# RWKV key direction: head norms summed into 16 rows and spread back by a zero-one matrix, b multiplied on GpSimd

## What is computed

```python
a = jax.nn.sigmoid((a0 + (xa @ a1) @ a2).astype(f32))
kk = (k * k_k.astype(f32)).reshape(B, T, RWKV_HEADS, RWKV_HEAD)
kk = kk / jnp.maximum(jnp.sqrt(jnp.sum(kk * kk, axis=-1, keepdims=True)), 1e-12)
k = k * (1.0 + (a - 1.0) * k_a.astype(f32))
...
# in the recurrence: -kk and b = kk * a
```

## Time and profile before

| what | value |
| --- | --- |
| median of 3 runs | 2409.98 us (2407.46 to 2410.36) |
| the profiled execution's own time | 2418.79 us |
| its span, first to last instruction | 2417.2 us |
| mean granted TensorE clock | 0.904 |
| busy in the span: PE, DVE, ACT, POOL | 87%, 41%, 28%, 7% |
| the block of the change in the trace | 1362.1 to 1433.7 us |

### The profile page before, as it was taken

The page is one execution under the profiler, slowest core; times in us unless marked ns, Lnnn a source line. Parts: engine busy times, 40 slices in busy tenths (PEclk is TensorE's granted clock), DMA queues, the critical chain, the costliest instruction groups (busy, mean ns, idle before and its releaser), DMA issues. The chain is left out here.

```text
span 2417.2 us, 51803 instructions
## 1 busy us (share of the span) xinstructions
PE 2112.1 (87%) x20994; PEld 1892.1 (78%) x20994; DVE 995.4 (41%) x1572; ACT 679.9 (28%) x1151; POOL 157.4 (7%) x240
## 2 busy tenths in 40 slices
PE   4599888878889999996699959999996789999995
PEld 4566556666689999996599739999873589999995
DVE  5323432211244333334943385544416643333333
ACT  2112335334223221221532233323201232212222
POOL 0002201333000000000000000000113000000000
PEclk7797899878999999998899759999977799999997
DMA  3022302455222323221132000001001222232311
GB/s 115 13 61 68 117 1 66 135 151 167 77 70 82 101 66 92 84 77 44 45 87 79 10 0 2 0 0 35 1 6 46 70 70 83 82 114 62 100 55 48
DMA packets 255006, 156.02 MB, mean 65 GB/s; under 512 B 24760, under 2 KB 247839, under 8 KB 254752
## 3 DMA queue, kind: packets, MB, share of 16 engines
q1 hardware_dynamic: 234644, 140.07, 19.6%
q10 hardware_dynamic: 14092, 7.95, 1.2%
q0 software_dynamic: 6144, 6.30, 0.9%
HBM read 148.89 MB, written 5.34 MB: 64 GB/s over the span
## 5 line engine op out<-in xcount | busy, mean ns | idle before, releaser
L308 PE MATMUL ps<-ffn_xh,ffn_wh 128*128 128x280 f32 x1408 | 299.1, 294 | 17.5 <-DVE ffn_xl L1394 13.2
L308 PE MATMUL ps<-ffn_xh,ffn_wl 128*128 128x280 f32 x1408 | 297.4, 293 | 0.0
L308 PE MATMUL ps<-ffn_xl,ffn_wh 128*128 128x280 f32 x1408 | 296.5, 292 | 0.0
L308 PEld LDWEIGHTS ps<-ffn_xh,ffn_wh 128*128 128x128 f32 x1408 | 226.1, 190 | 18.5 <-issue 18.3
L308 PEld LDWEIGHTS ps<-ffn_xh,ffn_wl 128*128 128x128 f32 x1408 | 225.8, 190 | 0.0
L308 PEld LDWEIGHTS ps<-ffn_xl,ffn_wh 128*128 128x128 f32 x1408 | 224.8, 190 | 0.0
L1296 ACT CAST ffn_wh<-wa 128x1024 fp32r<-128x1024 f32 x88 | 91.3, 1042 | 206.6 <-PE ps L308 179.5
L308 PE MATMUL ps<-ffn_hid_h,ffn_wh 128*128 128x280 f32 x704 | 148.0, 291 | 0.0
L308 PE MATMUL ps<-ffn_hid_h,ffn_wl 128*128 128x280 f32 x704 | 147.6, 291 | 0.0
L308 PE MATMUL ps<-ffn_hid_l,ffn_wh 128*128 128x280 f32 x704 | 147.5, 291 | 0.0
L314 DVE TENSOR_TENSOR ffn_wl<-wa,ffn_wh 128x1024 fp32r<-128x1024 f32 x88 | 107.6, 1225 | 85.8 <-ACT ffn_wh L1296 85.8
(11 more groups left out here) (356 smaller groups left out, 4000.3 us busy)
## 6 DMA issues: line engine op xcount, KB each, us to landing
wa<-in_ffn_w_gate SPq DMA_DIRECT2D x44, 512.0 KB, 3.6
wa<-in_ffn_w_up SPq DMA_DIRECT2D x44, 512.0 KB, 3.6
arena<-in_cache_latent SPq DMA_DIRECT2D x104, 128.0 KB, 2.1
wb<-in_ffn_w_down SPq DMA_DIRECT2D x16, 768.0 KB, 4.7
wb<-in_ffn_w_down SPq DMA_DIRECT2D x16, 640.0 KB, 4.2
wb<-in_cache_latent SPq DMA_DIRECT2D x73, 128.0 KB, 2.2
wa<-in_attn_w_o SPq DMA_DIRECT2D x8, 512.0 KB, 4.5
wa<-in_rwkv_w_r SPq DMA_DIRECT2D x8, 512.0 KB, 3.6
```

The lines of the kernel that those rows point to most:

```text
L308: mm = nc.tensor.matmul(dst[:, s, 0:HALF], a[:, c * width:(c + 1) * width], b[:, c, s * HALF:(s + 1) * HALF], start=first and n == 0, stop ...
```

## The change

- The square is taken straight from k with the scale k_k (L1671); the separate copy into kk goes.
- The sums of all 16 heads are collected in one tile of 16 rows: for each m a 128 x 16 window of a constant of zeros and ones puts the two heads of m into rows 2m and 2m + 1, and all eight m accumulate in one pair of banks (L1636). All eight go ahead of the other matmuls.
- Maximum, reciprocal and square root are taken once, on 16 x 560 (L1686, L1688, L1679). The square root stands between the sigmoids of m = 2 and m = 3.
- PE spreads the 16 rows back over 128 partitions with a 16 x 1024 matrix of zeros and ones (`spread`, a new input that SP fetches to a free weight buffer), one 16-row matmul per half and m (L1650). Ahead of it the products for the first four m are made; the rest alternate with it.
- DVE makes kk as (k * k_k) * spread in one instruction (L1695), out of PSUM, ahead of the product that overwrites k (L1698).
- b = kk * a is made on GpSimd (L1705).

The diff (the last part, which passes the new input, is left out):

```diff
@@ -71,7 +71,7 @@
 NCON = _at
 
 _at = LATER = CON["causal"][0]
-for _name, _n in [("abrb_t", 2 * L), ("near_t", L), ("owner", DB)]:
+for _name, _n in [("abrb_t", 2 * L), ("near_t", L), ("owner", DB), ("window", 4 * DC - 2)]:
     CON[_name] = (_at, _n)
     _at += _n
 NLATER = _at - LATER
@@ -116,7 +116,10 @@
     ang = (inv[:, None] * pos[None, :]).astype(np.float32)
     put("cos", np.concatenate([np.cos(ang), np.cos(ang)]))
     put("sin", np.concatenate([-np.sin(ang), np.sin(ang)]))
-    return c, later[:, LATER:LATER + NLATER]
+
+    put("window", np.arange(4 * DC - 2)[None, :] == 2 * (DC - 1) + p[:, None] // RH, later)
+    spread = np.repeat(np.eye(2 * DC, dtype=np.float32), RH, 1)
+    return c, later[:, LATER:LATER + NLATER], spread
 
 
 class Ring:
@@ -346,6 +349,11 @@
             dve.wait_ge(cut.slab_done, n + 1)
             x = split(xT[:, n])
             nc.vector.tensor_tensor(x, x, halves(2 * (n % 4)), ALU.add).then_inc(cut.kept, 1)
+
+        def head_window(m):
+
+            a = 2 * (DC - 1) - 2 * m
+            return const("window", P, a, a + 2 * DC)
 
         def ge(eng, s, v):
 
@@ -1602,76 +1610,100 @@
 
 
         sg, kk, av = mixed0, mixed1, xx
-        w2, a2 = wa.buf[0][0:64], wa.buf[1][0:64]
+        w2, a2, spread = wa.buf[0][0:64], wa.buf[1][0:64], wa.buf[2][0:2 * DC]
+        HD = 2 * DC
         sq = wb.buf[0][:, 0:2 * T].rearrange("p (s t) -> p s t", s=2)
         kscale = wb.buf[1][:, 0:2 * T].rearrange("p (s t) -> p s t", s=2)
-        norms = hT
+        inverse = rs[0:HD]
         one_less = wb.buf[1][:, 4 * T:4 * T + DC]
-        l2_in, sw_done, a_done, sw_kept, a_kept = sem("lora2_in"), sem("decay_done"), sem("a_done"), sem("decay_kept"), sem("a_kept")
-        kk_raw, kk_sq, kk_summed, kk_mean, kk_root, kk_done = (sem(f"kk_{n}") for n in ("raw", "squared", "summed", "mean", "root", "done"))
-        k_scaled, b_done, less = sem("k_scaled"), sem("b_done"), sem("one_less")
+        l2_in, spread_in = sem("lora2_in"), sem("spread_in")
+        sw_done, a_done, sw_kept, a_kept = sem("decay_done"), sem("a_done"), sem("decay_kept"), sem("a_kept")
+        kk_sq, kk_summed, kk_mean, kk_root, kk_spread, kk_done = (sem(f"kk_{n}") for n in ("squared", "summed", "mean", "root", "spread", "done"))
+        less, scale_done, k_scaled, b_done = sem("one_less"), sem("k_scale"), sem("k_scaled"), sem("b_done")
+        SUMS_AT, A_AT, W_AT, SPREAD_AT = 0, 2, 4, (6, 0)
         with nc.Block(no_gpsimd_drain=True) as block:
             @block.sync
             def _(sp):
+                sp.dma_start(a2, w["rwkv_a2"][0]).then_inc(l2_in, 16)
                 sp.dma_start(w2, w["rwkv_w2"][0]).then_inc(l2_in, 16)
-                sp.dma_start(a2, w["rwkv_a2"][0]).then_inc(l2_in, 16)
+                sp.dma_start(spread, w["spread"]).then_inc(spread_in, 16)
 
             @block.tensor
             def _(pe):
+                for m in range(DC):
+                    pe.wait_ge(kk_sq, m + 1)
+                    for s in range(2):
+                        mm = nc.tensor.matmul(ps[0:HD, SUMS_AT + s, 0:HALF], head_window(m), sq[:, m % 2, s * HALF:(s + 1) * HALF],
+                                              start=m == 0, stop=m == DC - 1)
+                    mm.then_inc(kk_summed, 1)
+
+                def second(m, bank, src, hid, done, left):
+                    ge(pe, left, m)
+                    for s in range(2):
+                        mm = nc.tensor.matmul(ps[:, bank + s, 0:HALF], src[:, m * P:(m + 1) * P],
+                                              lora[0:64, hid, s * HALF:(s + 1) * HALF], start=True, stop=True)
+                    mm.then_inc(done, 1)
+
+                def spread_out(m):
+                    ge(pe, kk_done, m - 1)
+                    for s in range(2):
+                        mm = nc.tensor.matmul(ps[:, SPREAD_AT[m % 2] + s, 0:HALF], spread[:, m * P:(m + 1) * P], inverse[:, s],
+                                              start=True, stop=True)
+                    mm.then_inc(kk_spread, 1)
+
                 pe.wait_ge(l2_in, 32)
+                FIRST = 4
+                for m in range(FIRST):
+                    second(m, A_AT, a2, 1, a_done, a_kept)
+                    second(m, W_AT, w2, 0, sw_done, sw_kept)
+                pe.wait_ge(spread_in, 16)
+                pe.wait_ge(kk_root, 1)
                 for m in range(DC):
-                    ge(pe, sw_kept, m)
-                    ge(pe, a_kept, m)
-                    for b, src, hid, done in ((0, w2, 0, sw_done), (2, a2, 1, a_done)):
-                        for s in range(2):
-                            mm = nc.tensor.matmul(ps[:, b + s, 0:HALF], src[:, m * P:(m + 1) * P],
-                                                  lora[0:64, hid, s * HALF:(s + 1) * HALF], start=True, stop=True)
-                        mm.then_inc(done, 1)
-                    pe.wait_ge(kk_sq, m + 1)
-                    ge(pe, kk_mean, 2 * (m - 1))
-                    for s in range(2):
-                        mm = nc.tensor.matmul(ps[:, 4 + 2 * (m % 2) + s, 0:HALF], pair, sq[:, m % 2, s * HALF:(s + 1) * HALF],
-                                              start=True, stop=True)
-                    mm.then_inc(kk_summed, 1)
+                    spread_out(m)
+                    if m + FIRST < DC:
+                        second(m + FIRST, A_AT, a2, 1, a_done, a_kept)
+                        second(m + FIRST, W_AT, w2, 0, sw_done, sw_kept)
 
             @block.scalar
             def _(act):
                 for m in range(DC):
-                    nc.scalar.activation(kk[:, m], k[:, m], ACT.Copy, scale=vcol("k_k", m)).then_inc(kk_raw, 1)
-                    act.wait_ge(kk_raw, m + 1)
                     ge(act, kk_summed, m - 1)
-                    nc.scalar.activation(sq[:, m % 2], kk[:, m], ACT.Square).then_inc(kk_sq, 1)
+                    nc.scalar.activation(sq[:, m % 2], k[:, m], ACT.Square, scale=vcol("k_k", m)).then_inc(kk_sq, 1)
+                for m in range(DC):
+                    act.wait_ge(a_done, m + 1)
+                    nc.scalar.activation(split(av[:, m]), halves(A_AT), ACT.Sigmoid, bias=vcol("a0", m)).then_inc(a_kept, 1)
                     act.wait_ge(sw_done, m + 1)
-                    nc.scalar.activation(split(sg[:, m]), halves(0), ACT.Sigmoid, bias=vcol("w0", m)).then_inc(sw_kept, 1)
-                    act.wait_ge(a_done, m + 1)
-                    nc.scalar.activation(split(av[:, m]), halves(2), ACT.Sigmoid, bias=vcol("a0", m)).then_inc(a_kept, 1)
-                for m in range(DC):
-                    act.wait_ge(kk_mean, 2 * m + 2)
-                    nc.scalar.activation(norms[:, m], norms[:, m], ACT.Sqrt).then_inc(kk_root, 1)
+                    nc.scalar.activation(split(sg[:, m]), halves(W_AT), ACT.Sigmoid, bias=vcol("w0", m)).then_inc(sw_kept, 1)
+                    if m == 2:
+                        act.wait_ge(kk_mean, 2)
+                        nc.scalar.activation(inverse, inverse, ACT.Sqrt).then_inc(kk_root, 1)
 
             @block.vector
             def _(dve):
                 ka = vec[:, VEC["k_a"][0]:VEC["k_a"][0] + DC]
                 nc.vector.tensor_scalar(one_less, ka, -1.0, 1.0, ALU.mult, ALU.add).then_inc(less, 1)
+                dve.wait_ge(kk_summed, DC)
+                nc.vector.tensor_scalar(inverse, ps[0:HD, SUMS_AT:SUMS_AT + 2, 0:HALF], 1e-24, None, ALU.max).then_inc(kk_mean, 1)
+                dve.wait_ge(kk_mean, 1)
+                nc.vector.reciprocal(inverse, inverse).then_inc(kk_mean, 1)
                 dve.wait_ge(less, 1)
                 for m in range(DC):
-
-                    dve.wait_ge(kk_summed, m + 1)
-                    nc.vector.tensor_scalar(split(norms[:, m]), halves(4 + 2 * (m % 2)), 1e-24, None, ALU.max).then_inc(kk_mean, 1)
-                    dve.wait_ge(kk_mean, 2 * m + 1)
-                    nc.vector.reciprocal(norms[:, m], norms[:, m]).then_inc(kk_mean, 1)
-
                     dve.wait_ge(a_kept, m + 1)
                     nc.vector.tensor_scalar(kscale[:, m % 2], av[:, m], vcol("k_a", m), one_less[:, m:m + 1], ALU.mult,
-                                            ALU.add).then_inc(k_scaled, 1)
-                    dve.wait_ge(k_scaled, 2 * m + 1)
-                    dve.wait_ge(kk_raw, m + 1)
+                                            ALU.add).then_inc(scale_done, 1)
+                    dve.wait_ge(kk_spread, m + 1)
+                    nc.vector.scalar_tensor_tensor(out=split(kk[:, m]), in0=split(k[:, m]), scalar=vcol("k_k", m),
+                                                   in1=halves(SPREAD_AT[m % 2]), op0=ALU.mult, op1=ALU.mult).then_inc(kk_done, 1)
+                    dve.wait_ge(scale_done, m + 1)
                     nc.vector.tensor_tensor(k[:, m], k[:, m], kscale[:, m % 2], ALU.mult).then_inc(k_scaled, 1)
+
+            @block.gpsimd
+            def _(pool):
                 for m in range(DC):
-                    dve.wait_ge(kk_root, m + 1)
```

(11 more changed lines are left out.)

## The result

The changed kernel takes 2430.36 us (median of 4 runs, 2424.55 to 2445.67), the kernel before 2408.72 (4 runs, 2405.12 to 2410.36). The ratio is 1.0092, interval [1.0052, 1.0132]: slower by 0.9%, where I had forecast 18 us less. The profiled execution took 2425.59 us, with a span of 2423.9.

What follows compares the result with a forecast made beforehand. Three bounds in turn: the fetch of w2 and a2, PE at 1.2 GHz, the DVE tail. Gains of 4.2, 8.9, 9.2 and 14.8 against costs of 4.0 and 14.8 give 18.3 us off 2409.98: 2391.7, range 2387 to 2407.

Steps and rivals of the forecast that it cites:

- the first part: What bounds the old block: weight fetch, PE at 1.2 GHz, DVE tail; any gain comes off the span one for one.
- the next block waits for something that it had for nothing: Rival, behind the block: the change does not do what it says; no gain, 2410 us; 3%.
- Sums first at 2.4 GHz: Block's start: PE begins at 1362.9 instead of 1367.06; eight groups of pair sums at 1.05 us take 8.4 us.
- the slow-clock rival: Whole block at clock 0.50, sums taking 16.2 us; gain only 3.2 us, 2406.8 us; 13%.
- Reciprocal at full length on 16 partitions: After the sums, on DVE: the single reciprocal takes the full 3.65 us, yet stays off the path.
- Root in the middle: Between sigmoids of m = 2 and m = 3: Sqrt and two table loads, no drain; 4.0 us around the root.
- Clock falls near the root and stays at 0.50: Between about 1378 and 1382 PE mostly waits, the clock falls and stays down; rounds take 6.19 us, spreading costs 14.8.
- L1692 beside GpSimd at no cost: Spreading rounds: DVE's scale is not slowed by GpSimd's b; DVE needs 1.95 us per m, b takes 1.36 to 1.43.
- the bounds of 0 and 5: Last four m: us lost in all if DVE's scale had to wait for each GpSimd b; 0 taken, upper bound 6%.
- the low end: Last four m: 0 us lost to GpSimd and DVE slowing each other, since POOL's median beside a busy DVE is 1.36.

Runs made afterwards that it cites:

- the seventh experiment: The changed kernel with 150 padding increments where PE waits anyway, and the square root replaced by a plain copy, so both table loads go: 2388.13 us (one run).
- the eighth experiment: The changed kernel with 150 padding increments where PE waits anyway, and low-rank and spreading matmuls over 128 rows, the added ones zeros: 2380.94 us, ratio 0.9893.
- the first experiment: The changed kernel with 150 semaphore increments on PE right ahead of the recurrence's loop: 2411.03 us, ratio 1.0012.
- the fifth: The changed kernel with 150 semaphore increments where PE waits anyway (25 and 65 in the projections, 60 ahead of the recurrence's loop): 2392.41 us, ratio 0.9940.
- the fourth: The kernel before with 150 semaphore increments on PE right ahead of the recurrence's loop: 2490.05 us, ratio 1.0336.

## Why the prediction was wrong

**The step that failed** is the last sentence of the first part: "A barrier stands between, so what the block gives back comes off the span one for one." It holds for time, and I took it to hold for everything. What the change did outside its block was to shift the code behind it. That the code moves was to be seen before the run: a compiled list can be counted, the page lists the queue of instruction fetches, and the trace shows rounds of 33.5 us without one fetch. What a shift of 52 would cost was not to be seen there. None of my rivals had it; "the next block waits for something that it had for nothing" (3%) comes near its effect, but says nothing of code, and was priced at no gain, not at a loss. It cost 33.0 us, and 34.0 in the kernel before with 52 increments.

**The block, step by step**, in us from its start (1362.1 in my timeline, 1353.1 in the trace):

| step | forecast | measured |
| --- | --- | --- |
| sums done | 9.2 | 8.8 |
| sigmoids of m = 2 done | 16.1 | 15.7 |
| first spreading group starts | 18.1 | 17.8 |
| sigmoid of a, m = 3, done | 20.1 | 19.7 |
| PE's last spreading group done | 51.0 | 50.0 |
| last b done | 53.3 | 55.4 |

- *Sums first at 2.4 GHz*: right. The clock stayed at 1.00 up to 1371, and the slow-clock rival is out.
- *Reciprocal at full length on 16 partitions*: right, 3.64 us against 3.65, and off the path.
- *Root in the middle*: right. The Sqrt starts 1.29 us after its load, as in the earlier trace rows, and the seventh experiment bounds all that the two loads cost at 2.7 us. By the Trainium skill's drain of 1.38 us per switch ("ScalarE: Activation LUTs", "What ACT_TABLE_LOAD costs") it would be 5.3, an estimate from that page's figures; the trace does not show it.
- *Clock falls near the root and stays at 0.50*: right in size, 0.50 from 1380 to 1409 with rounds of 6.19 us as in the earlier trace rows. The reason that I gave for the fall, that PE mostly waits there, is not needed. Without the root PE is busy 8.00 of 8 us and then 10.00 of 10, and the clock falls; with 128 rows PE has the same wait for the root (0.86 us in both), and the clock stays at 1.00 up to 1390. The rule of the Trainium skill ("TensorE: Matmul & The Clock Gate", "What's actually happening"), that activity releases the throttle, does not hold for the low-rank and spreading matmuls of this block. The prediction argued that from rows, and the eighth experiment shows it. Few rows alone do not bring the slow clock either: most matmuls of the recurrence are 64*64, and between 1480 and 1513.5 in the kernel before they run at 1.00, with PE busy 31.99 of 33.5 us. What sets the two apart stays open.
- *L1692 beside GpSimd at no cost*: mis-sized. It takes 1.61 to 1.62 us instead of 0.46, and L1705 1.80 instead of the 1.36 to 1.43 of the earlier trace rows, where GpSimd ran beside other DVE work. Each time L1692 starts 0.5 us behind L1705 and ends 0.3 behind it (1404.28 + 1.61 = 1405.89 beside 1403.78 + 1.80 = 1405.58 above), so it looks like a wait for GpSimd's operation rather than slower work. DVE's 1.95 us per m became 2.89, so in the last four groups DVE and not PE set the pace. Behind PE's last group came 5.4 us instead of 2.3; PE was done 1.0 earlier, and the end came 2.1 us later than forecast. That is within the bounds of 0 and 5 that I had given it; I took the wrong end. The reason that I gave for the low end, POOL's own median beside a busy DVE, said nothing on what DVE loses.

The block took 56.0 us for 53.3 (these 2.1, and 0.6 from the last result to the barrier's end), and with the loop in a good place the kernel took 2392.41 for 2391.7. The model of the block was right, the model of the program was not.

## What to carry to other kernels

A hand-scheduled program has one more resource: the place of its loops in the instruction stream. Where an edit changes the number of instructions ahead of a long loop, compare the packets of the instruction queue and the rounds of the loop before believing any verdict on the edit; if they moved, pad in an idle place on that engine and time again. And look whether matmuls over few rows that run at the slow clock can be filled up with zeros: here that alone took the block from 56.6 to 43.6 us.

## What the runs showed of the hardware that I had not expected

- A loop of 1702 PE instructions runs without a fetch from some places. From others it is fetched again in every second round (32 us over eight rounds) or in every round (72 us). The refetch stalls PE for 3.3 to 4.5 us at the jump back, and behind it the clock is at 0.50 for some 10 to 14 us.
- A semaphore increment on PE takes 0.152 us from start to start. I had counted on a third of it, the 0.051 of its own duration.
- DVE's scale of 560 elements takes 0.46 to 0.57 us alone and 1.61 to 1.62 with a GpSimd multiplication beside it (the multiplication on DVE itself takes 0.73). DVE's two-input products stay at 0.73 to 0.80, but none of them starts while GpSimd multiplies, so they do not show what such an operation would pay.
- In the last part of the recurrence PE is busy throughout and the clock falls to 0.50, sooner in some executions than in others. In the first experiment's profile:

```profile
1727.00:1747.00 20.00, 20.00 (x201) 17.14 (x201) 0.00 (x0) 0.37 (x1) 0.00 (x0) 0.57 0.01 2
```

and in the fifth's:

```profile
1727.00:1747.00 20.00, 20.00 (x338) 18.70 (x337) 2.03 (x4) 1.12 (x3) 0.00 (x0) 0.84 0.01 2
```

  That part took 134.8 us in the first and 119.9 in the fifth, where it had also begun earlier. A late beginning is not enough: in the fourth it began last, at 1771, and took 119.3. It may be why runs of one kernel lie up to 25 us apart (2388.91 to 2414.05 in the fifth). What decides it was not tried.
